# Quarter-row gather of an expert's context rows, and the order of the first expert's rows

## The chip, the cores and the metric

The kernel runs on one core of a Trainium2 chip. The metric is device time in microseconds (us) of one execution; lower is better. Times are medians over several executions, and one further execution was taken with the hardware profiler.

## What is computed

One step of a hybrid diffusion trunk, in float32. Its 128 context tokens and 1024 latent tokens go through the same layer: modulation, a token mixing part (a large input projection, a short convolution, a recurrence), and then a mixture of 16 experts. Each expert chooses tokens itself: it takes the 128 latent tokens and the 16 context tokens that have the highest affinity for it. The part that matters here, shortened from the reference:

```python
cap = EC_CAPACITY_FACTOR * T // N_EXPERTS        # 128 latent, 16 context
aff = jax.nn.softmax(einsum('btd,de->bte', h, w_router))
top_w, top_idx = lax.top_k(jnp.swapaxes(aff, 1, 2), cap)
xs = h[bidx, top_idx]
hid = jax.nn.silu(einsum('becd,edf->becf', xs, w_g)) * einsum('becd,edf->becf', xs, w_u)
ys = einsum('becf,efd->becd', hid, w_d) * top_w[..., None]
return jnp.zeros_like(h).at[bidx, top_idx].add(ys)
```

All widths (model and expert) are 1024.

## The kernel before

The program is a sequence of stages with a barrier between them. The stage before the experts makes the normalized rows h2, stores them in DRAM (`h2_d`, one row of 1024 numbers for each of the 1152 tokens), computes the affinities, and selects. The expert stage, which this change is about, starts at about 1699 us of the trace and ends at about 2553 us. There each engine has its own program, and semaphores tie them together.

**Slots.** Each of the three matrices of an expert (gate "g", up "u", down "d") is 4 MB and comes in four pieces of 1 MB, called slots here, 192 in all. `ORDER_W` (line 151) sets the order: g0 to g3 of expert 0, u0 to u3 of expert 0, then for each expert g of the next one, d of this one, u of the next one. SyncE (SP) loads slots into a ring `WF` of eight buffers, one load each time a slot has been used. A float32 product is made of three passes over rounded numbers: ScalarE (ACT) rounds the slot into `WH` (`high`, line 2082) and VectorE (DVE) makes the rest `WL` (`low`, line 2162); TensorE (PE) then multiplies high rows by high weights, low rows by high weights (line 2040), the context rows (line 2051), and high rows by low weights (line 2058). ACT and DVE run `LEAD` = 3 slots ahead.

**Rows.** For expert e, `places(e)` (PE, line 1982) turns one-hot matrices that DVE made (`one_hot`, line 2142) into token numbers and weights, and `numbers(e)` (DVE, line 2150) writes them to `IDX` and `TW`. Column 2 of `IDX` holds numbers of quarter rows: partition 32a + i has quarter a of context row i, for i below 16, and the other partitions point at spare rows behind the tokens. Until now the scatter of the results alone used that column. `fetch(e)` (POOL, line 1952) gathers 128 latent rows into `XG` and 16 context rows into `XC`, 16 partitions of 1024 numbers each. `rows_t(e)` (PE, line 1991) transposes XG in eight pieces of 128x128 and XC in eight pieces of 16x128. ACT (`rows_high`) and DVE (`rows_low`) bring the result into `XH`, `XL2` and `XCT`. PE does `rows_t(e + 1)` behind slot u1 of expert e, and `places(e + 2)` behind slot u2.

**Hidden rows.** `hidden_t(e)` (PE, line 2006) transposes the gated hidden rows: eight pieces of `SG`, 128x128, and two pieces of `SGC`, 128x128, which hold the 16 context rows in quarters on the four groups of 32 partitions. So the layout that the change brings to XC is in use for SGC already, and the down slots read it at line 2048.

**Start.** On DVE: `one_hot(0)`, `numbers(0)`, `one_hot(1)`, `numbers(1)`, `low` of slots 0 to 2, `rows_low(0)`. On PE: `places(0)`, `places(1)`, `rows_t(0)`, slot 0. Slot 0 also waits for `numbers(1)` (line 2027).

Of the kernel before, what the change touches and what calls it, by code (L numbers as in the profile page):

```python
# [16 lines left out]
P = 128  # L17
D = 1024
KT = D // P
# [3 lines left out]
T = TN * P  # L23
# [4 lines left out]
GW = 256  # L28
NE = 16
CAP_L = 2 * TL * P // NE  # L30
CAP_C = 2 * P // NE
# [47 lines left out]
def trunk(nc, x_prompt, x_sample, state, cond, c_ctx, w_ada, b_ada, norm1, w_in, conv_w, conv_b,  # L79
# [3 lines left out]
    with ctx:  # L83
# [16 lines left out]
        def scratch(name, shape):  # L100
            return nc.dram_tensor(name, shape, F32, kind="Internal").ap()
# [5 lines left out]
        sg_d = scratch("sg_d", [2, D, T])  # L107
        sg_flat = sg_d.rearrange("a d t -> (a d) t")
        x1_d = scratch("x1_d", [T + CAP_C, D])
        h2_d = scratch("h2_d", [T, D])  # L110


        PS = [ctx.enter_context(nc.psum_tensor(f"bank{i}", [P, 512], F32)) for i in range(8)]
# [6 lines left out]
        IDENT = CST[:, C_ID:C_ID + P]  # L120
# [1451 lines left out]
        with nc.Block() as block:  # L1572
            @block.sync
            def _(sp):
                for i, dst in enumerate((G1, SH2, A2)):
                    for c in range(2):
                        sp.dma_start(dst[:, c], mod_d[c, i].partition_broadcast(P)).then_inc(modv_in, 16)
                sp.dma_start(WR[:], w_router[0].rearrange("(k p) e -> p k e", p=P)).then_inc(wr_in, 16)
                for i, t in enumerate(ORDER):
                    if i >= 2:  # L1580
                        sp.wait_ge(x1_made, i - 1)
                    sp.dma_start(XL[:, i % 2], x_rows[t]).then_inc(xl_in[i % 2], 16)

                sp.dma_start(x1_d[T:T + CAP_C, :], x_prompt[0, 0:CAP_C, :]).then_inc(spare_in, 16)
                for q in range(4):
                    expert_rows(sp, q)

                sp.wait_ge(mix_mm, 2 * TN)
                sp.dma_start(MG[:], b_ada[0, 5 * D:6 * D].partition_broadcast(2)).then_inc(bg2_in, 16)
                for i in range(4):  # L1590
                    if i in (0, 2):

                        b = ADA + i // 2
                        if i:
                            sp.wait_ge(g2_mm, 1)
                        sp.dma_start(AWG[:], w_ada_v[:, :, b * 512:(b + 1) * 512]).then_inc(awg_in, 16)
                    expert_rows(sp, 4 + i)
                sp.wait_ge(spare_in, 16)

            @block.gpsimd  # L1600
            def _(pool):
# [276 lines left out]
        TW = ex("TW", [P, 2, NE])  # L1878
        TOK4 = ex("TOK4", [P, 1])
        XG = ex("XG", [P, D])  # L1880
        XC = ex("XC", [CAP_C, D])
        XH = ex("XH", [P, 2, KT, CAP_L], F32R)
        XL2 = ex("XL2", [P, 2, KT, CAP_L], F32R)
        XCT = ex("XCT", [P, 2, KT, CAP_C])
        SG = ex("SG", [P, D])
        SGC = ex("SGC", [P, GW])
        HH = ex("HH", [P, KT, CAP_L], F32R)
# [1 line left out]
        HC = ex("HC", [P, 2, P])  # L1889
# [2 lines left out]
        NR_ = 5  # L1892
        WH = ex("WH", [P, NR_, 2, D], F32R)
        WL = ex("WL", [P, NR_, 2, D], F32R)
        x1_quarters = x1_d.rearrange("t (a n) -> (t a) n", a=4)

        cx_in = sem("cx_in")
# [37 lines left out]
        with nc.Block() as block:  # L1935
# [14 lines left out]
            @block.gpsimd  # L1950
            def _(pool):
                def fetch(e):

                    pool.wait_ge(idx_made, 2 * e + 2)
                    if e:
                        pool.wait_ge(x_t, 3 * e)
                    pool.indirect_dma_start(XG[:], None, h2_d, bass.IndirectOffsetOnAxis(IDX[:, 0, e:e + 1], 0)) \
                        .then_inc(xg_in, 16)
                    pool.indirect_dma_start(XC[:], None, h2_d,
                                            bass.IndirectOffsetOnAxis(IDX[0:CAP_C, 1, e:e + 1], 0)) \  # L1960
                        .then_inc(xg_in, 16)

                def add_rows(e):
                    pool.wait_ge(ys_made, 3 * e + 3)
                    if e:
                        pool.wait_ge(y_out, 32 * e)
                    pool.indirect_dma_start(x1_d, bass.IndirectOffsetOnAxis(IDX[:, 0, e:e + 1], 0), YS[:], None,  # L1967
                                            compute_op=ALU.add).then_inc(y_out, 16)
                    pool.indirect_dma_start(x1_quarters, bass.IndirectOffsetOnAxis(IDX[:, 2, e:e + 1], 0), YC[:],
                                            None, compute_op=ALU.add).then_inc(y_out, 16)  # L1970

                fetch(0)
                fetch(1)
                for e in range(NE):
                    if e + 2 < NE:
                        fetch(e + 2)
                    add_rows(e)
                pool.wait_ge(y_out, 32 * NE)

            @block.tensor  # L1980
            def _(pe):
                def places(e):

                    pe.wait_ge(oh_made, e + 1)
                    for t in range(TL):
                        nc.tensor.matmul(PS[6][:, 384:389], OH[:, t, :], TB[:, t, e, :],
                                         start=(t == 0), stop=(t == TL - 1))
                    nc.tensor.matmul(PS[6][:, 392:397], OH[:, CTX, :], TB[:, CTX, e, :],
                                     start=True, stop=True).then_inc(place, 1)

                def rows_t(e):

                    pe.wait_ge(xg_in, 32 * e + 32)
                    if e:
                        pe.wait_ge(g_silu, 3 * e)
                    for h in range(2):
                        for k in range(4 * h, 4 * h + 4):
                            ins = nc.tensor.transpose(PS[h][:, (k % 4) * P:(k % 4 + 1) * P],
                                                      XG[:, k * P:(k + 1) * P], IDENT)
                        ins.then_inc(x_t, 1)  # L2000
                    for k in range(KT):
                        ins = nc.tensor.transpose(PS[6][:, GW + k * CAP_C:GW + (k + 1) * CAP_C], XC[:, k * P:(k + 1) * P],
                                                  IDENT[0:CAP_C, 0:CAP_C])
                    ins.then_inc(x_t, 1)

                def hidden_t(e):
# [11 lines left out]
                def slot(q):  # L2018
# [25 lines left out]
                    for kk in range(2):  # L2044
                        k = 2 * kp + kk
                        for j in range(4):
                            if kind == "d":
                                lhs = HC[:, k % 2, 32 * (k // 2):32 * (k // 2) + CAP_C]
                            else:
                                lhs = XCT[:, e % 2, k, :]  # L2050
                            nc.tensor.matmul(ctx_out[32 * j:32 * j + CAP_C, :], lhs,  # L2051
                                             WF[:, q % 8, kk, GW * j:GW * j + GW],
                                             start=(k == 0), stop=(k == KT - 1))
# [15 lines left out]
                pe.wait_ge(ctx_zero, 1)  # L2069
                places(0)  # L2070
                pe.wait_ge(idx_made, 2)
                places(1)
                pe.wait_ge(idx_made, 4)
                rows_t(0)
                for q in range(NQ):
                    if q == at("d", LAST, 0):
                        hidden_t(LAST)
# [3 lines left out]
            def _(act):  # L2081
# [37 lines left out]
                        act.wait_ge(g_ln, 2 * e + i + 1)  # L2119
                        nc.scalar.activation(b, b, ACT.Exp, scale=-1.0).then_inc(g_sig, 1)  # L2120

                for q in range(LEAD):
                    high(q)
                rows_high(0)
                for q in range(NQ):
                    kind, e, kp = ORDER_W[q]
                    if kind == "u" and kp == 2 and e < LAST:
                        rows_high(e + 1)
                    if kind == "g" and kp == 2 and e:
                        hidden_high(e - 1)  # L2130
                    if (kind, kp) == ("d", 0) and e == LAST:
                        hidden_high(e)
                    elif (kind, kp) == ("d", 0):
                        sigmoid(e + 1)
                    if (kind, e, kp) == ("u", 0, 0):
                        sigmoid(0)
                    if q + LEAD < NQ:
                        high(q + LEAD)

            @block.vector  # L2140
            def _(dve):
# [28 lines left out]
                def rows_low(e):  # L2170
                    for h in range(2):
                        dve.wait_ge(xh_made, 2 * e + h + 1)
                        nc.vector.tensor_tensor(XL2[:, e % 2, 4 * h:4 * h + 4], PS[h][:].rearrange("p (k n) -> p k n", k=4),
                                                XH[:, e % 2, 4 * h:4 * h + 4].bitcast(F32), ALU.subtract).then_inc(xl_made, 1)
                    dve.wait_ge(x_t, 3 * e + 3)
                    nc.vector.tensor_copy(XCT[:, e % 2], PS[6][:, GW:GW + KT * CAP_C].rearrange("p (k n) -> p k n", k=KT)) \
                      .then_inc(xl_made, 1)

                def hidden(e):
# [31 lines left out]
                one_hot(0)  # L2211
                numbers(0)
                one_hot(1)
                numbers(1)
                for q in range(LEAD):
                    low(q)
                rows_low(0)
                one_hot(2)
                dve.wait_ge(g2_in, 80)
                for q in range(NQ):  # L2220
# [110 lines left out]
```

## Time and profile before

| what | value |
|---|---|
| runs, median (lowest to highest) | 2590.4 us (2586.36 to 2593.39), 3 runs |
| the profiled execution: its time, its span | 2590.0 us, 2588.3 us |
| PE busy | 2425.6 us, 94% |
| DVE busy | 1427.0 us, 55% |
| ACT busy | 1138.7 us, 44% |
| POOL busy | 432.5 us, 17% |
| mean granted clock of TensorE | 0.966 |

The span is the time from the first to the last instruction in the trace. Busy shares are means over stages with different limits, so a stage is read by itself. Matmuls are pipelined and their ends are modelled; for the pace of PE one takes the distance of two starts, not a sum of durations. A granted clock of 1.00 is 2.4 GHz, 0.50 is 1.2 GHz.

### The profile page before, as it was taken

To read this page: it belongs to the slowest core of one execution; us is meant where nothing else is said; L and a number is where in the kernel's file an instruction comes from. 1 tells how busy PE (TensorE), PEld (TensorE's weight loads), DVE (VectorE), ACT (ScalarE), POOL (GpSimd) and SP (SyncE) were. 2 spreads that over 40 slices of the span, in tenths; PEclk is the share of its full clock that TensorE was granted. 3 is DMA by queue.
4 is the path that set the end of the run, shared out by engine and by line. 5 is a ranking of instruction groups with operands and counts; after the bars stand their busy time and mean duration, and the time that the engine had idled before them with its cause. 6 is when DMAs were issued, how large, how long until landed. Compare 5 with 4: busy or idle time off the path is not lost. (4 is left out here: it accounts for less than half of the span.)

```text
span 2588.3 us, 43370 instructions
## 1 busy us (share of the span) xinstructions
PE 2425.6 (94%) x16756; PEld 2015.8 (78%) x16756; DVE 1427.0 (55%) x2696; ACT 1138.7 (44%) x1861; POOL 432.5 (17%) x609
## 2 busy tenths in 40 slices
PE   7899999999999999999889989659999999999992
PEld 2399999999999999999889978336666666666661
DVE  2455464645455454645433344677677767776762
ACT  2454544444454544444312022135565555556552
POOL 0011110211111110211111124112112111211211
PEclk9899999999999999999999999869999999999996
DMA  6511112121211112121264234537888888888864
GB/s 242 205 44 58 55 51 65 35 72 38 77 43 61 52 52 64 35 72 38 78 224 151 73 119 136 214 127 255 266 275 271 279 268 273 278 270 276 268 196 164
DMA packets 222639, 376.95 MB, mean 146 GB/s; under 512 B 11851, under 2 KB 146283, under 8 KB 222480
## 3 DMA queue, kind: packets, MB, share of 16 engines
q1 hardware_dynamic: 206696, 326.32, 37.9%
q0 software_dynamic: 15776, 48.27, 6.7%
q8 instruction: 128, 2.10, 0.3%
q14 instruction: 29, 0.24, 0.0%
q10 hardware_dynamic: 10, 0.02, 0.0%
HBM read 329.97 MB, written 44.66 MB: 145 GB/s over the span
## 5 line engine op out<-in xcount | busy, mean ns | idle before, releaser
L722 PE MATMUL bank<-HT,W 128*128 128x384 f32 x5760 | 1046.9, 338 | 9.9 <-DVE bank L1219 9.9
L722 PEld LDWEIGHTS bank<-HT,W 128*128 128x128 f32 x5760 | 994.4, 188 | 13.3 <-DVE bank L1219 10.2
L2167 DVE TENSOR_TENSOR WL<-WF,WH 128x2048 fp32r<-128x2048 f32 x192 | 432.2, 2285 | 144.9 <-ACT WH L2087 144.9
L2087 ACT ACTIVATE WH<-WF 128x2048 fp32r<-128x2048 f32 x192 | 359.1, 1917 | 112.4 <-PE bank L2058 103.1
L1414 PE MATMUL bank<-YO,W 128*128 128x384 f32 x960 | 172.2, 337 | 18.9 <-ACT YO L1430 18.9
L1414 PEld LDWEIGHTS bank<-YO,W 128*128 128x128 f32 x960 | 168.5, 190 | 19.2 <-issue 19.2
L1967 POOL DMA_INDIRECT x_d<-YS,IDX x16 | 88.0, 5502 | 567.9 <-DVE YS L2205 567.9
L2040 PE MATMUL bank<-WH,XH 128*128 128x512 f32 x512 | 165.5, 404 | 3.1 <-issue 3.1
L2040 PE MATMUL bank<-WH,XL 128*128 128x512 f32 x512 | 161.1, 396 | 0.0
L2058 PE MATMUL bank<-WL,XH 128*128 128x512 f32 x512 | 154.8, 424 | 0.0
L2058 PEld LDWEIGHTS bank<-WL,XH 128*128 128x128 f32 x512 | 86.1, 188 | 66.9 <-issue 42.5
L2051 PE MATMUL bank<-WF,XCT 128*16 128x256 f32 x2048 | 135.9, 383 | 0.0
L1299 POOL TENSOR_TENSOR KH<-X 128x256 f32<-128x256 f32 x32 | 26.5, 836 | 538.7 <-DVE X L1066 368.2
L1051 DVE TENSOR_TENSOR W<-W_FULL,W 128x1024 fp32r<-128x1024 f32 x80 | 98.5, 1231 | 32.6 <-ACT W L858 32.4
L2040 PEld LDWEIGHTS bank<-WH,XL 128*128 128x128 f32 x512 | 97.2, 190 | 22.2
L2040 PEld LDWEIGHTS bank<-WH,XH 128*128 128x128 f32 x512 | 93.7, 190 | 23.0 <-issue 3.2
L1058 DVE TENSOR_SCALAR KK<-ZS,CWP 128x384 f32<-128x384 f32 x48 | 23.0, 480 | 147.2 <-ACT ZS L873 147.2
L2051 PEld LDWEIGHTS bank<-WF,XCT 128*16 128x16 f32 x2048 | 46.8, 96 | 72.0 <-issue 47.0
L1166 DVE TENSOR_SCALAR ON<-bank,RST 128x128 f32<-128x128 f32 x72 | 25.1, 349 | 128.9 <-ACT RST L985 128.9
L954 ACT ACTIVATE QR<-bank 128x384 f32<-128x384 f32 x48 | 23.6, 492 | 143.9 <-PE bank L722 143.9
L858 ACT ACTIVATE W<-W_FULL 128x1024 fp32r<-128x1024 f32 x80 | 83.7, 1047 | 0.0
L2040 PE MATMUL bank<-WH,HH 128*128 128x512 f32 x256 | 80.7, 396 | 1.5 <-ACT HC L2105 1.5
(246 smaller groups left out, 3397.5 us busy)
## 6 DMA issues: line engine op xcount, KB each, us to landing
WF<-in_w_e_gate_dram SPq DMA_DIRECT2D x64, 1024.0 KB, 4.9
WF<-in_w_e_up_dram SPq DMA_DIRECT2D x64, 1024.0 KB, 4.9
WF<-in_w_e_down_dram SPq DMA_DIRECT2D x64, 1024.0 KB, 5.6
W_FULL<-in_w_in_dram SPq DMA_DIRECT2D x80, 512.0 KB, 3.7
AW<-in_w_ada_dram SPq DMA_DIRECT2D x10, 2048.0 KB, 9.5
sg_d<-QR SPq DMA_DIRECT2D x48, 192.0 KB, 1.9
GL<-sg_d POOLq DMA_DIRECT2D x48, 192.0 KB, 2.6
ya_d<-CY SPq DMA_DIRECT2D x24, 192.0 KB, 1.9
```

What stands on the lines that cost most here:

```text
L722: ins = nc.tensor.matmul(bank[:, 0:CH], W[:, slot, a, k, :], HT[:, b, k, at * CH:(at + 1) * CH], start=(i == 0 and k == 0), stop=(i == 2 a ...
L858: nc.scalar.activation(W[:, slot, 0], W_FULL[:, slot, 1], ACT.Copy).then_inc(w_hi, 1)
L1051: nc.vector.tensor_tensor(W[:, slot, 1], W_FULL[:, slot, 1], W[:, slot, 0].bitcast(F32), ALU.subtract).then_inc(w_lo, 1)
L1166: nc.vector.tensor_scalar(ON[:, t % 2], PS[2 + t % 2][:, 0:P], RST[:], None, ALU.mult) \
L1299: nc.gpsimd.tensor_tensor(KH[:, k % 2, 0], xs[:, :, P:XW].to_broadcast([P, 2, P]), xs[:, :, 1:XW], ALU.subtract).then_inc(kh_diff, 1)
L1414: ins = nc.tensor.matmul(PS[j % 4][:, 0:CH], W[:, m, a, k, :], src[:, k, n * CH:(n + 1) * CH], start=(i == 0 and k == 0), stop=(i == 2 and ...
L1967: pool.indirect_dma_start(x1_d, bass.IndirectOffsetOnAxis(IDX[:, 0, e:e + 1], 0), YS[:], None, compute_op=ALU.add).then_inc(y_out, 16)
L2040: nc.tensor.matmul(PS[bank + h][:], part[:, k, :], WH[:, q % NR_, kk, 512 * h:512 * h + 512], start=(k == 0 and part is hi_), stop=False)
L2051: nc.tensor.matmul(ctx_out[32 * j:32 * j + CAP_C, :], lhs, WF[:, q % 8, kk, GW * j:GW * j + GW], start=(k == 0), stop=(k == KT - 1))
L2058: ins = nc.tensor.matmul(PS[bank + h][:], hi_[:, k, :], WL[:, q % NR_, kk, 512 * h:512 * h + 512], start=False, stop=(k == KT - 1))
L2087: nc.scalar.activation(WH[:, q % NR_], WF[:, q % 8], ACT.Copy).then_inc(h_made, 1)
L2167: nc.vector.tensor_tensor(WL[:, q % NR_], WF[:, q % 8], WH[:, q % NR_].bitcast(F32), ALU.subtract).then_inc(l_made, 1)
```

## The change

Context rows are gathered as 128 quarter rows of 256 numbers, by `IDX` column 2, into `XC` with the layout of `SGC`. `rows_t` then transposes them in two pieces of 128x128 in place of eight of 16x128; the copy to `XCT` takes 256 columns for 128; line 2047 reads XCT as it reads HC. `h2_d` gets 16 spare rows, which SP fills in the stage before by one more DMA (64 KB), since the unused partitions gather from there. At the start of the expert stage `rows_t(0)`, `rows_low(0)` stand ahead of `places(1)`, `numbers(1)` and of two of the three first slots' `low`.

```diff
-        h2_d = scratch("h2_d", [T, D])
+        h2_d = scratch("h2_d", [T + CAP_C, D])
...
                 sp.dma_start(x1_d[T:T + CAP_C, :], x_prompt[0, 0:CAP_C, :]).then_inc(spare_in, 16)
+                sp.dma_start(h2_d[T:T + CAP_C, :], x_prompt[0, 0:CAP_C, :]).then_inc(spare_in, 16)
...
-        XC = ex("XC", [CAP_C, D])
+        XC = ex("XC", [P, GW])
...
-        XCT = ex("XCT", [P, 2, KT, CAP_C])
+        XCT = ex("XCT", [P, 2, 2, P])
...
+        h2_quarters = h2_d.rearrange("t (a n) -> (t a) n", a=4)
...
-                    pool.indirect_dma_start(XC[:], None, h2_d,
-                                            bass.IndirectOffsetOnAxis(IDX[0:CAP_C, 1, e:e + 1], 0)) \
+                    pool.indirect_dma_start(XC[:], None, h2_quarters,
+                                            bass.IndirectOffsetOnAxis(IDX[:, 2, e:e + 1], 0)) \
                         .then_inc(xg_in, 16)
...
-                    for k in range(KT):
-                        ins = nc.tensor.transpose(PS[6][:, GW + k * CAP_C:GW + (k + 1) * CAP_C], XC[:, k * P:(k + 1) * P],
-                                                  IDENT[0:CAP_C, 0:CAP_C])
+                    for c in range(2):
+                        ins = nc.tensor.transpose(PS[6][:, GW + c * P:GW + (c + 1) * P], XC[:, c * P:(c + 1) * P], IDENT)
...
-                            if kind == "d":
-                                lhs = HC[:, k % 2, 32 * (k // 2):32 * (k // 2) + CAP_C]
-                            else:
-                                lhs = XCT[:, e % 2, k, :]
+                            lhs = (HC if kind == "d" else XCT[:, e % 2])[:, k % 2, 32 * (k // 2):32 * (k // 2) + CAP_C]
...
                 pe.wait_ge(idx_made, 2)
+                rows_t(0)
+                pe.wait_ge(xl_made, 3)
                 places(1)
-                pe.wait_ge(idx_made, 4)
-                rows_t(0)
...
-                for q in range(LEAD):
+                for q in range(LEAD - 1):
                     high(q)
                 rows_high(0)
+                high(LEAD - 1)
...
-                    nc.vector.tensor_copy(XCT[:, e % 2], PS[6][:, GW:GW + KT * CAP_C].rearrange("p (k n) -> p k n", k=KT)) \
+                    nc.vector.tensor_copy(XCT[:, e % 2], PS[6][:, GW:2 * GW].rearrange("p (c n) -> p c n", c=2)) \
...
                 one_hot(1)
+                low(0)
+                rows_low(0)
                 numbers(1)
-                for q in range(LEAD):
+                for q in range(1, LEAD):
                     low(q)
-                rows_low(0)
                 one_hot(2)
```

The start of the expert stage on PE, before: L1986 and L1988 are `places`, L1998 and L2002 `rows_t(0)`, L2040 opens slot 0.

```order
L1986 MATMUL bank<-TB,OH 128x5 x8
L1988 MATMUL bank<-TB,OH 128x5
L1986 MATMUL bank<-TB,OH 128x5 x8
L1988 MATMUL bank<-TB,OH 128x5
L1998 MATMUL bank<-CST,XG 128x128 x8
L2002 MATMUL bank<-CST,XC 128x16 x8
L2040 MATMUL bank<-WH,XH 128x512 x2
```

The same place on PE with the change, where these lines are L1988, L1990, L2000, L2004 and L2041.

```order
L1988 MATMUL bank<-TB,OH 128x5 x8
L1990 MATMUL bank<-TB,OH 128x5
L2000 MATMUL bank<-CST,XG 128x128 x8
L2004 MATMUL bank<-CST,XC 128x128 x2
L1988 MATMUL bank<-TB,OH 128x5 x8
L1990 MATMUL bank<-TB,OH 128x5
L2041 MATMUL bank<-WH,XH 128x512 x2
```

The transposes moved ahead of the second `places`, and the eight small ones became two.

The same stretch on DVE, before, from the one-hot matrices of expert 1 on: L2153 to L2160 are `numbers(1)`, L2167 is `low`, L2173 and L2176 are `rows_low(0)`.

```order
L2147 TENSOR_SCALAR OH<-CST,POST 128x128 x8
L2147 TENSOR_SCALAR OH<-CX,POST 128x128
L2153 TENSOR_REDUCE TW<-bank 128x1
L2154 TENSOR_SCALAR IDX<-bank 128x1
L2153 TENSOR_REDUCE TW<-bank 128x1
L2154 TENSOR_SCALAR IDX<-bank 128x1
L2157 TENSOR_SCALAR TOK_13225<-bank 128x1
L2160 TENSOR_TENSOR IDX<-TOK_13225,CX 128x1
L2167 TENSOR_TENSOR WL<-WF,WH 128x2048 x3
L2173 TENSOR_TENSOR XL_13229<-bank,XH 128x512 x2
L2176 COPY XCT<-bank 128x128
```

And with the change, where every one of these lines has a number lower by one.

```order
L2146 TENSOR_SCALAR OH<-CST,POST 128x128 x8
L2146 TENSOR_SCALAR OH<-CX,POST 128x128
L2166 TENSOR_TENSOR WL<-WF,WH 128x2048
L2172 TENSOR_TENSOR XL_13230<-bank,XH 128x512 x2
L2175 COPY XCT<-bank 128x256
L2152 TENSOR_REDUCE TW<-bank 128x1
L2153 TENSOR_SCALAR IDX<-bank 128x1
L2152 TENSOR_REDUCE TW<-bank 128x1
L2153 TENSOR_SCALAR IDX<-bank 128x1
L2156 TENSOR_SCALAR TOK_13226<-bank 128x1
L2159 TENSOR_TENSOR IDX<-TOK_13226,CX 128x1
L2166 TENSOR_TENSOR WL<-WF,WH 128x2048 x2
```

`rows_low(0)` moved ahead of `numbers(1)` and of two `low`, and its copy to XCT has twice the columns. In the other experts the order on every engine is as it was.

## Rows read from the trace of the kernel before

**Rows 1.** The page's first line

```profile
span 2588.3 us, 43370 instructions
```

**Rows 2.** Windows, PE alone: stretch, length, busy us, PEclk, DMA share, GB/s

```profile
1715.60:1719.80 4.20, 4.15 (x16) 0.51 0.47 140
1743.20:1751.00 7.80, 7.72 (x41) 0.56 0.33 130
1860.00:2500.00 640.00, 640.00 (x4673) 1.00 0.84 272
```

**Rows 3.** Waits from 1700 us on: total us, times, longest

```profile
PE bank L1998 <- DMA XC<-h_d,IDX: 3.0, 1, 3.0
PE bank L1998 <- DVE SGC L2195: 1.8, 1, 1.8
ACT WH L2087 <- PE bank L2058: 103.1, 64, 5.9
```

**Rows 4.** Timeline of PE, rows_t(2): start us, us, engine, line, operation

```profile
1796.04 1.21 PE L2058 MATMUL bank<-WL,XH 128*128 128x512 f32 x4
1797.09 1.03 PE L1998 MATMUL bank<-CST,XG 128*128 128x128 f32 x8
1798.06 0.67 PE L2002 MATMUL bank<-CST,XC 16*128 16x16 f32 x8
...
1799.24 0.63 PE L2040 MATMUL bank<-WH,XL 128*128 128x512 f32 x2
```

**Rows 5.** Timeline of PE, hidden_t(1), between the same kinds of matmuls

```profile
1813.94 1.21 PE L2058 MATMUL bank<-WL,XH 128*128 128x512 f32 x4
1814.98 1.03 PE L2011 MATMUL bank<-CST,SG 128*128 128x128 f32 x8
1815.86 0.38 PE L2015 MATMUL bank<-CST,SGC 128*128 128x128 f32 x2
...
1816.54 0.62 PE L2040 MATMUL bank<-WH,XL 128*128 128x512 f32 x2
```

**Rows 6.** Timeline of the start of the expert stage

```profile
1706.04 0.88 POOL L1959 DMA_INDIRECT XC<-h_d,IDX  x1 [0.30 <-issue]
...
1706.32 0.35 PE L1986 MATMUL bank<-TB,OH 128*128 128x5 bf16 x8 [2.76 <-DVE OH L2147]
...
1707.47 6.69 DVE L2167 TENSOR_TENSOR WL<-WF,WH 128x2048 fp32r<-128x2048 f32 x3
...
1709.67 1.94 PE L1998 MATMUL bank<-CST,XG 128*128 128x128 f32 x8 [2.97 <-DMA XC<-h_d,IDX]
...
1711.54 1.03 PE L2002 MATMUL bank<-CST,XC 16*128 16x16 f32 x8
1711.65 0.60 ACT L2094 ACTIVATE XH<-bank 128x512 fp32r<-128x512 f32 x1 [0.26 <-PE bank L1998]
...
1714.07 1.28 DVE L2173 TENSOR_TENSOR XL<-bank,XH 128x512 fp32r<-128x512 f32 x2
1715.27 0.28 DVE L2176 COPY XCT<-bank 128x128 f32<-128x128 f32 x1
...
1715.65 1.19 PE L2040 MATMUL bank<-WH,XH 128*128 128x512 f32 x2 [3.08 <-issue]
```

**Rows 7.** The XC gathers: shortest/median/longest ns of the POOL instruction, and us to landing

```profile
L1959 POOL DMA_INDIRECT XC<-h_d,IDX x16: 849/925/3161, 1706.0 to 2416.2; - x16
...
DMA to landing us min/median/max: 3.5/5.1/7.7
```

**Rows 8.** Timeline, the longest of those POOL instructions and DVE beside it

```profile
1754.74 3.16 POOL L1959 DMA_INDIRECT XC<-h_d,IDX  x1 [0.30 <-issue]
1754.90 2.28 DVE L2167 TENSOR_TENSOR WL<-WF,WH 128x2048 fp32r<-128x2048 f32 x1
```

**Rows 9.** Timeline, expert 3's rows: the copy to XCT, and places behind the next slot

```profile
1850.31 0.28 DVE L2176 COPY XCT<-bank 128x128 f32<-128x128 f32 x1
...
1853.50 0.36 PE L1986 MATMUL bank<-TB,OH 128*128 128x5 bf16 x8
```

More of the change, by code:

```diff
@@ L1597, in _ @@
                     expert_rows(sp, 4 + i)
-                sp.wait_ge(spare_in, 16)
+                sp.wait_ge(spare_in, 32)
             @block.gpsimd
```

## The prediction, made before the change was run

> **What bounds the kernel now.** The change sits in the expert stage, so I read that stage alone. First the windows: from 1860 to 2500 us PE is busy for 640.00 of 640 us at a granted clock of 1.00, while the DMA engines are at 0.84 [rows 2]. Then the waits: past 1700 us ACT waits for PE's last matmul of a slot 64 times, 103.1 us in all, and the long waits of PE itself before its transposes are single: 3.0 us for the first XC gather, 1.8 us for SGC of expert 0 [rows 3]. So TensorE's stream sets the pace, ACT and the weight loads follow it, and whatever time PE loses or wins between two slots moves the end. A busy PE is a modelled figure, so I take costs from distances between starts in the timeline [rows 4, 5]. The start of the stage is another matter: there PE waits, and the timeline [rows 6] shows who is late last. The sum is made against the profiled execution, 2590.0 us with a span of 2588.3 us [rows 1]; the median of the runs shown is 0.4 us above it.
>
> **The transposes of experts 2 to 15.** What must be priced is eight pieces of 16x128 against two of 128x128. Before: from the first low-weight matmul of slot u1 (1796.04) to the XL matmul of slot u2 (1799.24) it is 3.20 us, with eight transposes of XG and eight of XC between [rows 4]. The kernel already has the new form elsewhere: hidden_t makes eight transposes of 128x128 and then two more of 128x128 from a tile in the quarter layout, between the same kinds of matmuls, and there the distance is 1816.54 - 1813.94 = 2.60 us [rows 5]. The changed rows_t is that sequence exactly. So it is worth 3.20 - 2.60 = **0.60 us an expert**, at full clock. Fourteen experts (2 to 15) do it inside the PE-bound stretch: 14 x 0.60 = **8.4 us**.
>
> The Trainium skill's page "TensorE: Matmul & The Clock Gate", section "LDWEIGHTS (loading the stationary operand)", says that a weight load costs its columns (128 of them at 1.2 per ns), however few rows it has. By that rule the six loads that go are an estimated 6 x 107 ns = 0.64 us an expert, 9.0 us for the fourteen; I keep 0.60, since rows 4 and 5 measure the very sequences.
>
> **Expert 1.** Its transposes run where the clock is granted at 0.56, near 1.2 GHz, from 1743.20 us on [rows 2]. The first expert's rows show that level: XG's eight start at 1709.67 and XC's at 1711.54, so one 128x128 transpose takes (1711.54 - 1709.67) / 8 = 0.234 us, and the eight of XC 1.03 us [rows 6]. Two for eight is 1.03 - 2 x 0.234 = **0.56 us**.
>
> **The start.** Before, rows_low(0) starts at 1714.07, though the second XH was ready at 1711.65 + 0.60 = 1712.25: DVE was in three `low` from 1707.47 for 6.69 us [rows 6]. That queue is what the reorder removes; without it the smaller transposes would win nothing here. But a new chain stands in its place, because slot 0 still waits for numbers(1), which now stand behind rows_low(0). If the gather lands as before: PE starts its transposes at 1709.67; the second XH ends at 1712.25; the second XL (1.28 / 2 = 0.64) at about 1712.9; the copy to XCT, with twice the columns, takes 0.28 to 0.56 us, say 0.4, to 1713.3. Then places(1) on PE and numbers(1) on DVE: from 1706.32 to 1707.47, 1.15 us, before [rows 6]. Slot 0 would start at about 1714.6 with a hand-over, 1.0 us ahead of 1715.65. The one `low` that stays in front ends by 1706.32 + 6.69 / 3 = 1708.6 and is covered by the gather. `low` of slots 1 and 2 end by 1714.5 + 4.5 = 1719.0, and slot 0 itself takes PE past that.
>
> The unknown is the gather: 128 rows of 1 KB now, where 16 rows of 4 KB landed in 3.5 us, the shortest of its kind, with a median of 5.1 and a longest of 7.7 [rows 7]. Its issue stands at 1706.04, ahead of the transposes at 1709.67 [rows 6]. Below 3.5 us it can't help, since the XG gather is issued just before. At 3.5 us the start wins 1.0 us, at 7.7 us it loses 4.2 - 1.0 = 3.2 us. I take half a microsecond of lateness, nearest to the 3.5 us of this very place, where no weights are being loaded: **0.5 us** won.
>
> **Costed at nothing.** The longer copy to XCT in the other experts: it starts at 1850.31, PE needs it at 1853.50 for places, and PE will be there 0.6 us sooner [rows 9]; 2.3 us remain, so 0.28 us more is covered. If that cover were gone, it would cost 14 x 0.28 = 3.9 us. The later gathers: fetch of an expert is issued one expert ahead (1754.74 for rows used at 1797.09 [rows 8, 4]), 42 us for a landing of at most 7.7. The context matmuls read 16 columns of a 256-column tile as the down slots do. The spare rows of h2_d are one more DMA on SP in the stage before, ahead of weight loads that have until the expert stage. The `high` that ACT does after rows_high(0): ACT has time from 1712.25 on. fetch(1) waits for the later numbers(1), 1 us later, needed 30 us on. POOL's queue holds nothing that anybody waits for in that time.
>
> **Sum.** 8.4 + 0.56 + 0.5 = 9.5 us; 2590.0 - 9.5 = 2580.5, and against the median 2590.4 it is **2580.9 us**, 0.37% faster. About 0.3% (7.8 us, a time of 2582.6) is what a measurement of this kernel can tell from no change, so the forecast lies only 1.7 us beyond that line, and the three runs before are 7 us apart.
>
> **Rivals.**
> - *The first gather is held up.* One XC issue took 3161 ns where the median is 925 [rows 7], and DVE was in a `low` from 0.16 us after its start [rows 8]. The new order puts `low(0)` right at the XC issue of the first expert, 1706.04. Against it: only one of sixteen was that long. If it happens, PE starts its transposes 3.16 - 0.88 = 2.3 us later, and the total is 9.5 - 2.3 = 7.2 us: 2583.2. The skill's page "SBUF — State Buffer", section "Who interferes with whom", says that a DVE instruction with two SBUF inputs blocks a GpSimd instruction that reads SBUF, whichever starts first holding the port. `low` has two such inputs; by that rule, the one long row agrees and the fifteen others leave it open. Chance 0.14.
> - *The clock falls or rises elsewhere.* PE's granted clock was 0.51 in slot 0 and 0.56 for 7.8 us from 1743.20 [rows 2], each time after PE had waited. The second stretch costs about 7.8 x 0.44 = 3.4 us. The change moves the start and its gaps, so one such stretch may be missing (2580.9 - 3.4 = 2577.5) or longer (2584.3). Chance 0.14, shared evenly.
> - *The gain is swallowed.* PE finishes rows_t sooner and waits at places for the copy, or in slot 0 for a gather of 7.7 us. For all of the 8.4 us to go, the copy would have to come 2.3 + 0.6 us later in each expert, against rows 9. Time 2590.4 - 0.5 = 2589.9. Chance 0.08.
> - *Slower: the weight stream.* Each expert's gather is now 128 KB in 1 KB pieces for 64 KB, beside loads that hold the DMA engines at 0.84 [rows 2]. It decides once a weight slot lands so late that PE waits more than the 0.60 us won, in every expert; at 1.2 us of waiting it is 14 x (1.2 - 0.6) = 8.4 us lost: 2598.8. Against it: 64 KB more is 0.24 us at 272 GB/s, once in 50 us, and ACT's waits are for PE [rows 3]. Chance 0.04.
> - *The change doesn't do what it says*, the transposes not being shorter: this is the third rival's time, and rows 5 speak against it.
>
> **How the numbers follow.** The forecast has the remaining 0.60. The range reaches from the case with one clock stretch missing, 2577.5, less a microsecond and a half for the scatter of runs, to 2588, which takes in a held-up gather, the 7.7 us landing (9.5 - 3.7 = 5.8 us won, 2584.6) and a longer clock stretch, but leaves out the two last cases. Faster by over 0.3%: the forecast for three quarters of its chance, since the line is so near (0.46), the better clock case (0.07), and half of the held-up gather (0.07): 0.60. Slower by over 0.3%: 0.04. Within: 0.36.
>
> **What would show it.** In the trace after, the distance from the low-weight matmul of u1 to the XL matmul of u2 should be 2.60 us; the pace from one expert to the next 0.6 us shorter; XC's transposes two of about 272 ns. Slot 0 should start between 1714.6 and 1715.2, with the XC gather landing within 4.4 us. A wait of PE for the copy at places, a POOL issue of 3 us at the start, an expert pace unchanged, or a DMA wait on ACT before `high` would prove me wrong, each for one rival.

## The result, and the profile after

| | median | lowest to highest | runs |
|---|---|---|---|
| changed kernel | 2575.8 us | 2571.68 to 2577.0 | 5 |
| kernel before, all runs of this comparison | 2586.36 us | 2584.75 to 2593.39 | 5 |

The ratio is 0.9947, with a 95% interval of 0.993 to 0.9964: 13.7 us faster, and between 9.3 and 18 us. That is the distance of the two means (2588.2 and 2574.6 us); the medians in the table are 10.6 us apart. The forecast was 9.5 us faster. The predicted time, 2580.9 us, was 5.1 us too high, and the measured one lies 0.2 us below the range. The three runs of before shown ahead of the prediction had a median of 2590.4 us; with two more it is 2586.36, and later comparisons gave 2587.4 (23 runs) and 2586.79 (11 runs).

The page of the changed kernel opens so, against [rows 1]:

```profile
span 2570.7 us, 43179 instructions
```

The two profiled spans differ by 17.6 us, more than the runs do, so the first question is where in the trace they part. The windows of PE, from 1860 us to the last experts, with the columns of [rows 2]:

```profile
1860.00:2480.00 620.00, 620.00 (x4507) 1.00 0.83 277
```

PE is busy without a gap at full clock, as before. The timeline of PE at rows_t(2), the stretch that [rows 4] shows of before:

```profile
1788.44 1.21 PE L2056 MATMUL bank<-WL,XH 128*128 128x512 f32 x4
1789.49 1.04 PE L2000 MATMUL bank<-CST,XG 128*128 128x128 f32 x8
1790.36 0.38 PE L2004 MATMUL bank<-CST,XC 128*128 128x128 f32 x2
...
1791.04 0.62 PE L2041 MATMUL bank<-WH,XL 128*128 128x512 f32 x2
```

From the low-weight matmul to XL's it is 1791.04 - 1788.44 = 2.60 us, where it was 3.20. That is the forecast to the hundredth, and it is the distance of hidden_t [rows 5]. The start of the expert stage in the timeline, against [rows 6] and [rows 7]:

```profile
1701.77 3.18 POOL L1961 DMA_INDIRECT XC<-h_d,IDX  x1 [0.30 <-issue]
1701.82 2.28 DVE L2166 TENSOR_TENSOR WL<-WF,WH 128x2048 fp32r<-128x2048 f32 x1
1706.81 1.94 PE L2000 MATMUL bank<-CST,XG 128*128 128x128 f32 x8 [7.52 <-DMA XC<-h_d,IDX]
...
1708.54 0.64 PE L2004 MATMUL bank<-CST,XC 128*128 128x128 f32 x2
...
1710.02 0.41 DVE L2175 COPY XCT<-bank 128x256 f32<-128x256 f32 x1
1710.49 0.38 PE L1988 MATMUL bank<-TB,OH 128*128 128x5 bf16 x8 [1.32 <-DVE XCT L2175]
...
1712.00 1.19 PE L2041 MATMUL bank<-WH,XH 128*128 128x512 f32 x2 [1.11 <-DVE IDX L2159]
```

The first XC issue takes 3.18 us where it took 0.88, and PE now has nothing to do before that gather lands: it is idle for 7.52 us, where `places(1)` used to stand in the middle of the wait. The chain that follows is the predicted one: the copy, places(1), numbers(1), slot 0. Of the waits of PE past 1695 us, the one of [rows 3] before the transposes of expert 1:

```profile
PE bank L2000 <- DVE SGC L2194: 1.8, 1, 1.8
```

The pause of 1.8 us before the transposes of expert 1 is still there. But behind it the clock behaved differently. The windows of PE, for the 8 us from those transposes on, are of the changed kernel:

```profile
1739.30:1747.30 8.00, 8.00 (x67) 1.00 0.50 178
```

and of the kernel before:

```profile
1743.28:1751.28 8.00, 8.00 (x42) 0.57 0.32 126
```

The fourth number is the granted clock: 1.00 against 0.57, and 67 matmuls done against 42.

I cut the traces at marks that all of them have. "Stage" is the issue of the expert stage's first DMA (1699.32 us before), "T1", "T2", "T15" are the first XG transposes of these experts, "end" the last group of low-weight matmuls. The columns give distances in us. The kernels in the lower rows are those of the experiments; all of them are one trace each.

| trace | start to stage | stage to slot 0 | slot 0 to T1 | T1 to T2 | T2 to T15 | T15 to end |
|---|---|---|---|---|---|---|
| before | 1699.3 | 16.3 | 27.6 | 53.8 | 659.6 | 80.4 |
| before, second trace | 1699.1 | 16.3 | 27.7 | 53.8 | 659.6 | 80.5 |
| start order alone | 1697.1 | 16.8 | 27.6 | 53.8 | 659.6 | 80.4 |
| changed | 1694.9 | 17.1 | 27.3 | 50.2 | 651.9 | 78.8 |
| changed, second trace | 1701.5 | 17.0 | 27.4 | 51.8 | 651.9 | 77.3 |
| new gather alone | 1694.3 | 16.5 | 27.5 | 51.8 | 651.9 | 79.8 |

Of the 17.6 us, 4.4 lie ahead of the expert stage, where the programs do the same but for one DMA of 64 KB. The start lost 0.7 us and won 0.3 back. T1 to T2 gave 3.6 where 0.6 was forecast, T2 to T15 7.6 = 13 x 0.59, and the last expert 1.6, of which 0.6 is its transposes and 1.0 the clock: a stretch at 0.50 near the end was 3.4 us long here and 6.8 us before. That last part is chance. The column goes from 77.3 to 80.1 us over the thirteen traces of this study with the new gather, and from 77.9 to 80.5 over the five with the old one. Slot 0 to T1 also varies by up to a microsecond between traces of the same program. Behind the end mark the difference is 0.8 us.

### The profile page after: what moved, and what is told of

Same layout as the page of the kernel before. It is cut to its first block and busy times, and to the rows that moved or that the text cites. A ratio compares the mean times of both kernels' runs of the same rounds, so it can differ in the third digit from the quotient of the medians.

```text
span 2570.7 us, 43179 instructions
## 1 busy us (share of the span) xinstructions
PE 2409.3 (94%) x16660; PEld 2004.9 (78%) x16660; DVE 1428.5 (56%) x2696; ACT 1138.2 (44%) x1861; POOL 438.1 (17%) x609
## 5 line engine op out<-in xcount | busy, mean ns | idle before, releaser
L2041 PE MATMUL bank<-WH,XH 128*128 128x512 f32 x512 | 164.0, 401 | 1.1 <-DVE IDX L2159 1.1
L2041 PE MATMUL bank<-WH,XL 128*128 128x512 f32 x512 | 159.8, 393 | 0.0
L2041 PEld LDWEIGHTS bank<-WH,XL 128*128 128x128 f32 x512 | 96.7, 189 | 21.8
L2041 PEld LDWEIGHTS bank<-WH,XH 128*128 128x128 f32 x512 | 93.2, 189 | 20.4 <-issue 1.2
L2041 PE MATMUL bank<-WH,HH 128*128 128x512 f32 x256 | 80.7, 396 | 1.5 <-ACT HC L2103 1.5
```

Of the source, the lines that this page charges most:

```text
L2041: nc.tensor.matmul(PS[bank + h][:], part[:, k, :], WH[:, q % NR_, kk, 512 * h:512 * h + 512], start=(k == 0 and part is hi_), stop=False)
```

## Experiments

**Both kernels again, and each half of the change by itself.** First the two kernels unchanged, for a measure of chance.

> The kernel before, unchanged, for a second trace and more times. If the profiled pair shown (2588.3 against 2570.7 us of span) owes part of its 17.6 us to chance, then this trace's stretch before the expert stage differs from 1699.3 us by some microseconds, and its time lies anywhere in 2584 to 2594 us. The pace from one expert to the next must be 50.74 us again. If the half-clock stretch behind the first expert's pause (1743 to 1751 us) is fixed by the program, it is there again; if it is a matter of chance, it may be missing.

Measured: 2584.8 us (2579.09 to 2589.82, 11 runs), ratio 0.9986 (0.9976 to 0.9995). So the very same program came out 0.14% apart from itself, beyond its own interval, and differences of that size between kernels mean little here. Its trace agrees with the first one in the table to 0.25 us in every column.

> The changed kernel, unchanged, for a second trace and more times. Theory: 8.8 us of the gain (transposes) are fixed, the start is about even because the first XC gather's issue takes 3.2 us, and the rest is chance; then the ratio to before comes nearer to 0.9966 than the 0.9947 seen, some 2575 to 2580 us. Rival: the new order at the start also keeps the clock up behind the pause of expert 1, worth 3 us more in every run; then the stretch is at full clock again here and the ratio stays at 0.995.

Measured: 2574.47 us (2574.07 to 2579.23, 5 runs), ratio 0.9954 (0.9941 to 0.9967); against the repeated kernel before it is 10.3 us by the medians and 9.0 by the means. Neither theory was quite right: the clock fell this time behind the pause, but for a shorter stretch. The windows of PE in the second trace of the changed kernel, from its T1 on:

```profile
1745.94:1753.94 8.00, 8.00 (x52) 0.79 0.35 130
```

The mean clock is 0.79, where it was 0.57 before, and T1 to T2 is 51.8 us. So even when the clock falls, expert 1 gives 2.0 us and not 0.56.

The new gather alone, with the old order on the three engines:

```diff
                 pe.wait_ge(idx_made, 2)
-                rows_t(0)
-                pe.wait_ge(xl_made, 3)
                 places(1)
+                pe.wait_ge(idx_made, 4)
+                rows_t(0)
...
-                for q in range(LEAD - 1):
+                for q in range(LEAD):
                     high(q)
                 rows_high(0)
-                high(LEAD - 1)
...
                 one_hot(1)
-                low(0)
-                rows_low(0)
                 numbers(1)
-                for q in range(1, LEAD):
+                for q in range(LEAD):
                     low(q)
+                rows_low(0)
```

> The quarter-row gather and the two transposes alone, with the old order at the start. Theory: all of the fixed gain but that of the start, 14 x 0.60 + 0.6 = 9.0 us less than before (ratio 0.9965), slot 0 opens about 16.3 us after the stage's first DMA issue as before, since the three low parts hide the transposes, and the first XC issue is about 1 us, since no low part stands beside it. Rival (the start order matters for the clock): the half-clock stretch of expert 1 is back and costs 3 us against the changed kernel.

Measured: 2574.3 us (2571.58 to 2577.55), ratio 0.9952 (0.9938 to 0.9967). It is as fast as the whole change: the gather and the transposes carry all of the gain. The timeline of this kernel's first XC gather:

```profile
1701.06 0.97 POOL L1961 DMA_INDIRECT XC<-h_d,IDX  x1 [0.30 <-issue]
```

128 pieces are issued in 0.97 us, 0.09 more than 16 pieces [rows 6]; they are not what made it 3.18.

The order of the start alone, on the kernel before (the same edits the other way round):

> The order of the start alone, with the old gather of 16 whole rows and eight small transposes. Theory: expert pace 50.74 us as before; the first XC issue takes about 3.2 us as in the changed kernel if low(0) beside it is the cause, and slot 0 opens up to 1.5 us later than before; the time is within 2 us of before. Rival (the length of the issue comes from 128 pieces in place of 16): the issue is 0.9 us and slot 0 opens 0.5 us sooner than before.

Measured: 2586.86 us (2579.26 to 2592.03, 12 runs), ratio 0.9997 (0.9987 to 1.0007): no difference. The timeline at the first XC gather, with the old 16 pieces:

```profile
1703.81 3.08 POOL L1959 DMA_INDIRECT XC<-h_d,IDX  x1 [0.30 <-issue]
1703.86 2.28 DVE L2168 TENSOR_TENSOR WL<-WF,WH 128x2048 fp32r<-128x2048 f32 x1
```

The issue is long here too, with DVE's `low` 0.05 us behind its start. So the order made it long and not the pieces, and slot 0 opened 0.5 us later than before, where the theory allowed 1.5.

**Taking low(0) away from the gather's issue.** The edit on DVE, on the changed kernel:

```diff
                 one_hot(1)
-                low(0)
                 rows_low(0)
                 numbers(1)
-                for q in range(1, LEAD):
+                for q in range(LEAD):
                     low(q)
```

> The changed kernel with low(0) of DVE moved behind numbers(1), so that no low part stands beside the first XC issue. Theory (the low part beside it lengthens the issue, 3.2 us in the changed kernel, 3.1 with the old gather in the new order, 1.0 with the new gather in the old order): the first XC issue takes about 1.0 us, and slot 0 opens at +15.9 us from the stage's first DMA issue in place of +17.0; the time falls by about 1 us. Rival (the issue is long for another reason, or the chain behind the gather is what counts): slot 0 opens at +17.0 again.

Measured: the first issue is back at about 1 us and slot 0 opens at 1707.71 - 1691.89 = 15.8 us after the stage's first DMA, 1.2 us sooner than in the changed kernel and 0.5 us sooner than before. The timeline:

```profile
1691.89 0.35 SPq L1940 DMA_DIRECT2D CX<-in_shape_constants_dram  x1
...
1698.71 0.97 POOL L1961 DMA_INDIRECT XC<-h_d,IDX  x1 [0.30 <-issue]
...
1707.71 1.19 PE L2041 MATMUL bank<-WH,XH 128*128 128x512 f32 x2 [1.11 <-DVE IDX L2159]
```

The times, 2575.18 us (2570.03 to 2577.84) and a ratio of 0.9956 (0.9943 to 0.9969), can't show one microsecond; the trace can. The Trainium skill's page "SBUF — State Buffer", section "Who interferes with whom", has the rule that the prediction cited: a DVE instruction with two inputs in SBUF contends with a GpSimd instruction that reads SBUF. The first gather fits it in all eighteen traces of this study: 3.08 to 3.18 us in the eleven with `low(0)` beside it, 0.88 to 0.97 us in the seven without. But most of the later gathers do not. For experts 3 to 14 the XC issue has a `low` starting 0.09 to 0.12 us behind it, as here in the kernel before:

```profile
1805.56 0.92 POOL L1959 DMA_INDIRECT XC<-h_d,IDX  x1 [0.30 <-issue]
1805.66 2.28 DVE L2167 TENSOR_TENSOR WL<-WF,WH 128x2048 fp32r<-128x2048 f32 x1
```

All 216 such issues in the eighteen traces took 0.91 to 1.05 us. The long ones have `low` starting between 0.01 us ahead and 0.05 us behind (the first gather), or 0.15 to 0.18 us behind (expert 2's, 3.15 to 3.29 us in sixteen traces); in the two traces where expert 2's issue is short, 0.95 us, `low` starts 0.18 us behind. Expert 1's issue, in the thirteen traces where a `low` has begun 1.2 us ahead of it and is still running, takes 1.8 to 1.9 us. So a `low` beside the issue goes with a longer one in three places and not in the others; a few hundredths of a microsecond go with the one or the other, and what decides stays open. Nor does the order of starts tell who waits: in all but one of the cases above 3 us POOL's instruction started first, and yet `low` took its usual 2.28 us and POOL was the one held up.

**Taking PE's pause away.** The pause before T1 comes from silu(0), which stood behind a `low` that waits for ACT:

```diff
-                    if (kind, e, kp) == ("u", 0, 1):
+                    if (kind, e, kp) == ("u", 0, 0):
                         silu(0)
```

> The changed kernel with silu(0) of DVE one step earlier, ahead of the low part that waits for ACT. PE's 1.76 us wait before the transposes of expert 1 should go, and with the pause the half-clock stretch behind it (none, 3.0 and 3.4 us long in three traces of kernels with the new gather): from slot 0 to those transposes 25.6 us in place of 27.3 to 27.5, and from there to the next expert's 50.2 us. 2 to 3.5 us less than the changed kernel. If the clock falls for another reason than the pause, 51.8 us stays and only 1.8 us are won.

Measured: 2574.2 us (2570.18 to 2574.89), ratio 0.9948 (0.9935 to 0.9961). In the trace PE goes from the slot into the transposes without a wait:

```profile
1740.79 1.21 PE L2056 MATMUL bank<-WL,XH 128*128 128x512 f32 x4
1741.84 1.03 PE L2000 MATMUL bank<-CST,XG 128*128 128x128 f32 x8
```

T1 to T2 is 50.15 us, the value of every later expert, and the clock is 1.00. Slot 0 to T1 is 26.4 us, 0.9 to 1.0 less than the changed kernel and not the forecast 1.8; part of it went into how long slot 0 ran at half clock.

> low_late and silu_early together: the sum of both, 3 to 4.5 us less than the changed kernel, so a ratio of 0.994 or less to the kernel before.

Measured: 2572.29 us (2568.05 to 2577.94, 6 runs), ratio 0.9944 (0.993 to 0.9959). Slot 0 opens at 15.7 us, slot 0 to T1 is 26.0, T1 to T2 50.2. Compared piece by piece that is 1.3 to 1.4, 1.3 to 1.5, and 0 to 1.7 us less than the changed kernel, and the median is the lowest of the kernels that ran more than once. The forecast ratio of 0.994 or less was just missed, and the intervals overlap, so by the measured times it is not shown to be faster than the change.

**Why the clock comes back sooner.** One reading: transposes right behind the pause keep the clock from returning, so with 16 of them it stays low longer than with 10. To test it I added transposes for expert 1 alone, first of the large form:

```diff
-                    for c in range(2):
+                    for c in [0, 1] * (4 if e == 1 else 1):
```

> The changed kernel, where for expert 1 alone the two XC transposes are done four times over (eight of 128x128, the same result written again). Theory: behind PE's pause the clock comes back only when the matmuls of slot u2 have run for a while, and transposes ahead of them hold that up; then the half-clock stretch is 6.8 us again as in the three traces with the eight small transposes, and from the transposes to the next expert's it is 53.2 us or more. Rival (the stretch's length is chance, or goes by time alone): 3 us or none again, and that distance is 51.8 + 6 x 0.23 = 53.2 at most, or 50.2 + 0.7 = 50.9 us.

Measured: 2575.79 us (2572.26 to 2579.75), T1 to T2 50.85 us. The clock did not fall at all, so the length of a stretch could not be seen; the run says nothing for the theory, and the distance is that of the rival.

Then eight of the small form, ahead of the two:

```diff
+                    for k in range(KT if e == 1 else 0):
+                        nc.tensor.transpose(PS[6][:, GW + k * CAP_C:GW + (k + 1) * CAP_C], XC[0:CAP_C, 0:P],
+                                            IDENT[0:CAP_C, 0:CAP_C])
                     for c in range(2):
```

> The changed kernel with eight more transposes of 16x128 for expert 1 alone, ahead of its two of 128x128 (they write a place that the two then overwrite). Theory (transposes right behind PE's pause hold the clock down): the half-clock stretch is 6.8 us again as in the three traces with the old gather, and from the transposes to the next expert's it is 53.8 us or more. Rival (old and new differ there by chance): 3.4 us or none, and that distance is 50.2 + 0.7 = 50.9 or 51.8 + 1.0 = 52.8 us.

> The same kernel as small_one a second time, for a second trace of that stretch. Theory: 53.8 us or more again; rival: another value.

Measured, in one execution each: 50.94 and 50.93 us, at full clock in both. The theory's 53.8 did not come, again because the clock stayed up. From the other side, the kernel before with only two of expert 1's eight small transposes (the rest is left out):

```diff
-                    for k in range(KT):
+                    for k in range(2 if e == 1 else KT):
```

> The kernel before, where for expert 1 alone only two of the eight small XC transposes are done; it leaves out six eighths of that expert's context rows. Theory: the half-clock stretch falls to 3.4 us or none, and the distance from these transposes to the next expert's from 53.8 to 51.8 us or less, though it saves 6 x 0.13 = 0.8 us of transposes only. Rival: 53.8 - 0.8 = 53.0 us.

> The same kernel as few_one a second time, for a second trace. Theory: 51.8 us or less; rival: 53.0 us or another value.

Measured: 51.91 and 51.87 us from T1 to T2, where the rival had 53.0. The clock fell in both, and came back early. The windows of the first, from its T1 on:

```profile
1740.73:1748.73 8.00, 8.00 (x51) 0.79 0.31 125
```

It is the 0.79 of the changed kernel's second trace, with the old gather and the old order.

That left one doubt: whether the clock falls seemed to be a matter of chance, and the sets were compared across programs. So I lengthened the pause until the clock had to fall, in two kernels that differ by nothing but the eight small transposes that the edit before the last adds:

```diff
+        pad = sem("pad")
...
                     if (kind, e, kp) == ("u", 0, 1):
+                        for i in range(3):
+                            nc.vector.tensor_tensor(YS[:], G2[:], G2[:], ALU.mult).then_inc(pad, 1)
+                            dve.wait_ge(pad, i + 1)
                         silu(0)
```

> The changed kernel with three more DVE products of 128x1024 ahead of silu(0), each waited for, so that PE's pause before the transposes of expert 1 grows from 1.76 to about 5 us. Its ten transposes follow. The pause should now bring the clock down in every trace. Theory (the stretch's length goes with the transposes that come first): the half-clock part from the transposes on is about 3.4 us or ends within slot u2, and from the transposes to the next expert's it is about 52 us. Rival: its length is the same as in the kernel with more transposes.

> The same kernel as pause_ten_1, for a second trace of that stretch: theory about 52 us from the transposes to the next expert's, rival the value of the kernel with more transposes.

> As pause_ten_1, with eight more transposes of 16x128 for expert 1 ahead of its two of 128x128. Theory: the half-clock part lasts about 3.4 us longer than with ten transposes, about 55 us from the transposes to the next expert's. Rival (only the pause counts): the distance grows by the transposes' own 1.0 us at half clock and by nothing else.

> The same kernel as pause_more_1, for a second trace of that stretch: theory about 55 us from the transposes to the next expert's, rival 1.0 us more than with ten transposes.

Measured, T1 to T2: 51.66 and 51.61 us with ten transposes, 53.85 and 53.75 us with eighteen. The pause was 5.53 us in all four. The windows from T1 on, of the first kernel with ten:

```profile
1744.44:1752.44 8.00, 8.00 (x52) 0.81 0.10 11
```

and of the first with eighteen:

```profile
1743.17:1751.17 8.00, 8.00 (x43) 0.59 0.01 3
```

From T1 to the first matmul of slot u2 it is 2.0 us with ten transposes and 3.2 with eighteen, so the eight take about 1.15 us themselves. 2.1 to 2.2 us were lost, so the clock's later return costs about another 1.0 us. The full clock came back 3.1 and 3.0 us behind T1 with ten, and 6.6 and 6.2 us behind it with eighteen. The theory's direction holds in all four traces; its 55 us was too high by 1.2. One rival is left: no run put ordinary matmuls of the same length where the eight transposes are, so it isn't shown that the clock came back later because they are transposes.

## Where the prediction was right, and where it was wrong

The time lay 0.2 us outside the range. Of the 5.1 us by which the predicted time was too high, 4.0 are the base (2590.4 against 2586.36 us), and 1.1 are left for the gain (9.5 against 10.6 us of the medians). The step of the argument that failed is the term of expert 1, 0.56 us, and the sign of the term of the start was wrong as well; the large term, 8.4 us, was right.

**The transposes of experts 2 to 15: right.** 0.60 us each from rows 4 and 5; measured 0.59, by the 13 distances from T2 to T15 (659.57 - 651.94 = 7.63 us). All five traces with the old gather and all thirteen with the new one give these two sums to the hundredth. It was worth pricing the new sequence by one that the kernel already had, and not by durations of single matmuls: eight small ones stand in the trace at 1.03 us at half clock, but how much of a small one hides behind its neighbour no duration says. The rule of weight loads in the Trainium skill's page "TensorE: Matmul & The Clock Gate", section "LDWEIGHTS (loading the stationary operand)", gave an estimated 0.64 us, a little high against the 0.59 measured.

**Expert 1: the mechanism that I priced was too small.** The term of 0.56 us measured 2.0 us when the clock fell and 3.6 when it did not. Of the 2.0, the transposes themselves are 0.5 (from T1 to slot u2's first matmul it is 2.53 us before and 2.01 in the changed kernel's second trace), so that price was right; the rest is the half-clock stretch, which ended 7.2 us behind T1 before and 3.4 us behind it there. The step that failed was to take the half-clock stretch as given and to price the transposes within it at its pace. Rows 2 show a mean of 0.56 over 7.8 us, and I listed a missing stretch as a rival and shared its chance evenly between better and worse. It was not even. All three traces with the old gather's 16 transposes have 53.8 us there, all eight with ten behind a pause, of either length, lie between 50.2 and 51.9, and the pair with the forced pause shows that the number of transposes moves it. Whether the clock falls at all did not follow their number (three of four traces with sixteen, four of six with ten, none of two with eighteen, all with the kernel's own pause), so the 3.6 us of the first trace are in part luck. The better side of that rival came true, for a reason that I had not given.

**The start: the forecast was wrong, its first rival right.** In place of 0.5 us won, slot 0 opened 0.7 us later. The first issue was held up, as the rival said (3.18 us, its rows 7 had 3.161), but its price was 1.5 us (11.88 - 10.35, from the stage's first DMA to the first transposes) and not 2.3, since the landing came quicker behind the issue. The prediction weighed it by one long row in sixteen and said that the fifteen others leave the rule open. They do not: twelve of them have a `low` starting 0.09 to 0.11 us behind and took 0.91 to 0.94 us. What counted was where exactly `low(0)` would start, and in all eleven traces with the new order and `low(0)` in it the issue was long. Without it the reorder wins the half microsecond: slot 0 at 15.8 us against 16.3.

**The base.** The sum was set against three runs whose median was 2590.4 us. More runs give 2586.4 to 2587.4, and the repeated kernel before 2584.8, so the base was 3 to 5.6 us too high. By parts the change is worth 7.6 + 0.6 + (2.0 to 3.6) - 0.7 = 9.5 to 11.1 us, and 12.1 with the last expert's microsecond; the first comparison gave 13.7 by the means and 10.6 by the medians, the two repeated kernels 9.0 and 10.3. What the 13.7 has beyond the parts is not explained by them; the two comparisons differ by 4.7 us of the means, so much of it can be chance. The 4.4 us ahead of the stage in the first pair of traces can't be put down to the change: that part lies anywhere between 1691.9 and 1701.5 us in the thirteen traces of kernels that do the same there. Their mean is 1695.7 us against 1698.1 in the five with the old gather, and 2.0 us of this difference are there by 90 us of the trace, where the programs are equal. Whether it is chance isn't shown. The lower end of the range took one missing stretch and 1.5 us of scatter, and needed a base that was not itself 3 us or more too high.

**Costed at nothing: right.** The longer copy took 0.41 us for 0.28, places did not wait for it (but in the start, where `places(1)` stands behind it by design), and no wait of ACT for a weight load appeared. The weight stream did not become the bound, and the transposes were really shorter. None of the other rivals came.

**What stays open.** Why the clock falls behind the 1.76 us pause in some traces and not in others (7 against 5 of those here) isn't settled: the three traces with added transposes kept it up, and all five with the old gather lost it. What makes the XC issue of expert 2 long in sixteen traces and short in two isn't settled either; it is long in one trace and short in the other of the very same kernel, the one with eight small transposes added.

## What to carry to other kernels

Price a new sequence by the same sequence elsewhere in the trace, start to start between the same neighbours: here 0.60 us was forecast and 0.59 measured, in each of thirteen distances from one expert to the next. When work is taken out just behind a pause of TensorE, ask how long the clock stays low with it and without it, for that may be worth more than the work. And when DVE work is moved, look at which descriptor issue of POOL it now stands beside.

## What the runs showed of the hardware

**The more transposes stand behind a pause, the later the full clock comes back.** With a forced pause of 5.53 us and ten transposes behind it, the granted clock over the next 8 us was 0.81 in both traces; with eighteen it was 0.59 and 0.61. With the kernel's own pause of 1.76 us and a clock that fell, it was 0.79 in four traces with ten transposes and 0.57 in three with sixteen. With the forced pause the full level came back 1.1 and 0.9 us into the matmuls that follow ten transposes, and 3.4 and 3.1 us into those that follow eighteen. The Trainium skill's page "TensorE: Matmul & The Clock Gate", section "Part 4: PE-mode transpose", says that transposes don't count as TensorE being busy in the way matmuls do; by that rule a burst of them behind a pause should delay the full clock, and these traces agree, though none of them tells transposes from ordinary matmuls in that place. Where the clock was at full level, transposes ran at its pace: ten took 1.04 us behind the changed kernel's own pause, from the first one's start to the next matmul's, and 2.0 us at half clock.

**A POOL gather's issue can triple.** An XC issue took 0.88 to 0.97 us at the stage's start without a two-input DVE product beside it. It took 3.08 to 3.18 us with one starting within 0.05 us of it, for 16 and for 128 pieces alike, and 3.15 to 3.29 us with one starting 0.15 to 0.18 us behind. But it took 0.91 to 1.05 us with one starting 0.09 to 0.12 us behind. Issuing 128 quarter rows of 1 KB took 0.09 us more than issuing 16 rows of 4 KB at the stage's start. They landed about as soon: a median of 5.0 us against 5.1, and at the stage's start 3.6 to 3.8 us against 3.4 to 3.5, where the issue was short.
